# Hybrid encoder layer: a pair of token blocks re-ordered, first loads split around a wait, waits on one engine folded

## The reference

```python
proj = x @ w_in                       # conv GLU | q | k | v | q_mem | gate logits
y_conv = conformer_conv(glu_in, ...)  # GLU, depthwise conv of 31, LayerNorm, silu, projection
y_attn = windowed_gqa(q, k, v, ...)   # 8 heads, +-128 tokens, bias, sink -> projection
y_mem  = memory_attention(q_mem, mem, w_mem_kv) @ w_mem_out
merged = g0 * y_conv + g1 * y_attn + g2 * y_mem          # g = sigmoid(gate logits + b)
x = layer_norm(ALPHA * x + merged @ w_o, ln1_g, ln1_b)
gate, up = split(x @ w_ffn_in)        # 1024 -> 2 x 2816
x = layer_norm(ALPHA * x + (silu(gate) * up) @ w_ffn_out, ln2_g, ln2_b)
```

## Time and profile before

| what | value |
|---|---|
| runs | 978.34, 979.25, 1060.41 us, median 979.25 |
| profiled execution | 978.15 us, of which the slowest core's span is 977.1 us and 1.05 us lie around it |
| spans of the 8 cores | 975.5 to 977.1 us |
| TensorE matmul busy | 932.3 us, 95% of the span |
| VectorE | 632.1 us, 65% |
| ScalarE | 436.6 us, 45% |
| GpSimd | 256.1 us, 26% |
| chain that ended last | 84% TensorE, 5% VectorE, 4% issue, 3% DMA |

### The profile page before, as it was taken

One profiled execution on the slowest core, in us unless ns is written; L12 is line 12 of the kernel. 1 busy time (PEld: TensorE's weight loads), 2 busy tenths in 40 slices (PEclk: granted clock), 3 DMA queues, 4 the chain that ended last, 5 costly groups with the idle time before them and its releaser, 6 DMA issues.

```text
span 977.1 us, 16482 instructions; the slowest of 8 cores (975.5 to 977.1 us)
## 1 busy us (share of the span) xinstructions
PE 932.3 (95%) x5405; PEld 437.2 (45%) x5501; DVE 632.1 (65%) x1050; ACT 436.6 (45%) x719; POOL 256.1 (26%) x280
## 2 busy tenths in 40 slices
PE   4999999999999999999999999999999999999895
PEld 1455544544444444444445444444444444444342
DVE  1323575666766857566668798966575676675776
ACT  1125657575663354444556467654001444442121
POOL 3200000112135334334332355434100233332000
PEclk9999999999999999999999999999999999999998
DMA  8997033474249999622487277775533323221312
GB/s 131 184 172 140 24 86 95 82 129 72 45 72 138 113 149 126 84 66 54 90 254 272 62 173 168 137 184 122 170 129 108 108 88 111 89 81 37 115 44 87
DMA packets 39684, 112.13 MB, mean 115 GB/s; under 512 B 4976, under 2 KB 16888, under 8 KB 38608
## 3 DMA queue, kind: packets, MB, share of 16 engines
q0 software_dynamic: 11104, 41.16, 29.5%
q1 hardware_dynamic: 28496, 69.91, 23.3%
HBM read 132.49 MB, written 30.47 MB: 167 GB/s over the span
## 4 chain that ended last, share of the span: by engine, by line
PE 84%; DVE 5%; issue 4%; DMA 3%; ACT 3%; POOL 1%; DVEq 0%; ACTq 0%; POOLq 0%; SPq 0%
PE ps L233 82%; DMA arena<-xt 2%; DMA arena<-w_bf_cache 1%; ACT arena L597 1%; ACT arena L645 1%; DVE arena L1446 1%; PE ps L1276 1%; DVE arena L1209 1%; POOL arena L147 0%; DVE arena L1509 0%; DVE arena L590 0%; DVE arena L1483 0%; ACT arena L600 0%; PE ps L760 0%; ACT arena L1191 0%
## 5 line engine op out<-in xcount | busy, mean ns | idle before, releaser
L233 PE MATMUL ps<-arena 128*128 128x512 bf16 (+5 forms) x4995 | 914.3, 358 | 34.5 <-DMA arena<-xt 13.9
L233 PEld LDWEIGHTS ps<-arena 128*128 128x128 bf16 (+2 forms) x5091 | 417.0, 98 | 516.3 <-issue 74.4
L1325 ACT COPY arena<-ps 128x512 f32<-128x512 f32 x132 | 76.3, 586 | 132.3 <-PE ps L233 132.2
L1335 POOL TENSOR_TENSOR arena<-arena 128x512 bf16<-128x512 f32 x66 | 89.0, 1349 | 143.2 <-DVE arena L1328 137.5
L1328 DVE TENSOR_TENSOR arena<-arena,ps 128x512 f32<-128x512 f32 x132 | 88.2, 684 | 39.1 <-PE ps L233 38.7
L940 POOL TENSOR_TENSOR arena<-arena 128x512 f32<-128x512 f32 (+1 forms) x48 | 63.9, 1338 | 104.2 <-DVE arena L931 104.2
L1191 ACT ACTIVATE arena<-arena 128x1024 bf16<-128x1024 f32 x26 | 27.5, 1058 | 95.5 <-DVE arena L1620 88.5
L931 DVE SCALAR_TENSOR_TENSOR arena<-arena,ps 128x512 f32<-128x512 f32 x72 | 49.2, 684 | 23.9 <-ACT arena L927 18.0
L1205 POOL TENSOR_TENSOR rs<-mvt,eps_t 128x1 f32<-128x1 f32 x32 | 24.7, 771 | 144.5 <-DVE mvt L1201 91.9
L923 DVE TENSOR_TENSOR arena<-arena,ps 128x512 f32<-128x512 f32 x54 | 37.0, 686 | 35.3 <-ACT arena L920 19.7
L920 ACT COPY arena<-ps 128x512 f32<-128x512 f32 x54 | 31.6, 585 | 55.8 <-PE ps L233 55.8
(11 more groups left out here) (118 smaller groups left out, 573.2 us busy)
## 6 DMA issues: line engine op xcount, KB each, us to landing
arena<-w_bf_cache SPq DMA_DIRECT2D x44, 512.0 KB, 4.5
arena<-u_scratch SPq DMA_DIRECT2D x64, 135.0 KB, 3.4
arena<-x SPq DMA_DIRECT2D x16, 512.0 KB, 13.6
y_scratch<-arena SPq DMA_DIRECT2D x16, 512.0 KB, 6.2
arena<-y_scratch SPq DMA_DIRECT2D x16, 512.0 KB, 5.4
out<-arena SPq DMA_DIRECT2D x15, 512.0 KB, 2.6
arena<-w_f POOLq DMA_DIRECT2D x22, 256.0 KB, 5.0
arena<-w_g POOLq DMA_DIRECT2D x9, 512.0 KB, 20.5
```

The source lines that it names most:

```text
L233: return pe.run(lambda: nc.tensor.matmul(out, lhsT, rhs, start=start, stop=stop, skip_group_check=onto), deps, inc)
L1325: return act.run(lambda: nc.scalar.copy(buf, ps[:, b, :]), deps)
L1335: return pool.run(lambda: nc.gpsimd.tensor_tensor(out=dst, in0=up, in1=gate, op=ALU.mult), deps)
```

## The change

Four edits; the work that is computed stays the same.

1. `wait` first reduces the list of tokens: of one engine, or one DMA slot, only the largest stays, and one semaphore instruction is issued for it.
2. GpSimd issues only glu(0,1) and xt 0, then does its memsets and masks, then waits until glu(0,1) has landed, and then issues the other nine loads in the same order.
3. Of block 9 only the add and the squares stay in `f2_block`; the tiny steps (`small`), `center` and `scale` become three items of `fill`, and `form_T4(6, 11)` becomes the fourth, ahead of the six sums.
4. In the last pair the order p1, p2, p6, p5, p3, p7 becomes p1, p5, p2, p6, p3, p7. Block 14's row passes are split: center stays on VectorE and is put ahead of p7's `acc`; the scaling goes to ScalarE (an Identity with a scale, 128x1024, f32), the addition of the table to GpSimd (128x1024, f32).

```diff
     def wait(self, deps):
+        last = {}
         for tok in _flat(deps):
+            k = id(tok[1] if tok[0] == "E" else tok[0])
+            if k not in last or last[k][-1] < tok[-1]:
+                last[k] = tok
+        for tok in last.values():
...
     load_glu(0, 1)
     load_xt(0)
-    load_glu(0, 0)
-    load_glu(1)
-    load_xt(1)
-    load_glu(2)
-    load_glu(3)
...
     t_vm1 = pool.run(lambda: nc.gpsimd.memset(vm129[:, :, :, 128:129], 1.0))
+
+    pool.wait([t_glu[0, 1]])
+    load_glu(0, 0)
+    load_glu(1)
+    load_xt(1)
+    load_glu(2)
+    load_glu(3)
...
+        if last:
+            z, r5 = p5()
+            filler(1)
+        p2()
+        filler(2 if last else 1)
+        r6 = p6()
+        if not last:
+            filler(2)
+            z, r5 = p5()
         filler(3)
...
             stats(tb)
+            center, scale = pair_rows(tb)
+            center()
             p7()
             t = r8 = acc(Xb, L, x, [hb_tok[tb + 1]])
             banks.release(x, t)
-            for f in pair_rows(tb):
-                f()
+            t_row = act.run(lambda: nc.scalar.activation(Xa, Xa, AF.Identity, scale=rs16[:, 16 + tb:17 + tb]),
+                            [pair_tok["y", tb, 0], pair_tok["rs", tb]])
+            t_row = pool.run(lambda: nc.gpsimd.tensor_tensor(out=Xa, in0=Xa, in1=ln2t[1], op=ALU.add), [t_row])
+            dma(sp, out_d[tb * 128:(tb + 1) * 128, :], Xa, s_out[tb % 3], [t_row])
             w, dw = banks.alloc(1)
...
     f2_block(8)
     form_T4(0, 6, mid_done)
-    form_T4(6, 11, mid_done)
-    rows = [f2_block(9)]
+    rows = f2_block(9) + [lambda: form_T4(6, 11, mid_done)]
     counts = (1, 1, 2, 1, 2, 2)
```

More of the change, by code:

```diff
@@ L1541, in f2_pair, with p2, p6, p5 @@
         filler(0)
[L1542 to L1554, removed]
+        def p2():
+            y, dy = banks.alloc(1)
+            t = product(y, lambda j: actT[11 + j][:, a], lambda j: w2[11 + j][:, L], True, [dy])
+            t = acc(Xa, L, y, [t, r1], 1.0, sm[tb][0])
+            banks.release(y, t)
+            h[tb] = [t]
+            square(tb, 0, Xa, L, t)
+        def p6():
+            t = product(x, lambda j: S[:, 1, j], lambda j: T2[:, j], False, [r1, forms("T2"), sa["2"]])
+            return acc(Xa, H, x, [t, hb_tok[tb]])
+        def p5():
+            z, dz = banks.alloc(1)
+            t = product(z, lambda j: S[:, 0, j], lambda j: T1j[j], True, [dz, forms("T1"), sa["1a"], sa["1b"]])
+            return z, acc(Xb, H, z, [t, hb_tok[tb + 1]])
+        if last:
[7 more added lines that the diff above has]
+            z, r5 = p5()
         filler(3)
@@ L1614, in pair_rows @@
         return out
+    f2_t = {}
     def f2_block(tb, hooks={}):
@@ L1624, in f2_block, with small, center, scale @@
         t_st2 = ln_stats(xb, [t_h], tb)
[L1625 to L1630, removed]
+        def small():
+            t3 = f2_t["var", tb] = ln_tiny(t_st2, tb, hsum[:, 1, tb:tb + 1], 0)
+            f2_t["rs", tb] = ln_rstd(t3, tb, rs16[:, 16 + tb:17 + tb])
+        def center():
+            f2_t["y", tb] = ln_center(xb, ln2t[0], tb, [f2_t["var", tb], e_state["ln2"]])
+        def scale():
+            t_ln = ln_scale(xb, xb, rs16[:, 16 + tb:17 + tb], ln2t[1], [f2_t["rs", tb], f2_t["y", tb]])
             hb_free[r] = [dma(sp, out_d[tb * 128:(tb + 1) * 128, :], xb, s_out[r], [t_ln])]
@@ L1633, in rows @@
                 load_hb(tb + 3)
-        if tb in (7, 9):
-            return rows
-        rows()
+        if tb == 9:
+            return [small, center, scale]
+        small()
+        if tb == 7:
+            return lambda: (center(), scale())
+        center()
+        scale()
     def y_stores():
```

## The result

The changed kernel takes 972.42 us (median of 5 runs, 971.61 to 973.03), the kernel before 979.19 us (median of its runs beside them). The ratio is 0.9935 [0.9921, 0.9950]: 6.4 us faster by the ratio, 5 to 8 by its interval, which counts as the same within 2%. Forecast were 972.8 us and a range of 969.0 to 976.5. Runs in which the cores of a die fall behind, as in the 1060.41 us of the kernel before, are left out of every ratio.

The account below looks back on a forecast made before the run. TensorE was taken as the bound, the least helped core setting the time: core 1's 976.1 us less 2.89 + 0.9 + 0.9 gives 971.4, plus 1.05 around the span 972.5; forecast 972.8 us, range 969.0 to 976.5.

Parts of the forecast that it names:

- Pair 10's pause: TensorE's 2.89 us wait for r1 until 919.62 us disappears once form_T4(6, 11) and block 9's passes move: -2.89 us.
- the margin at p3: In pair 10, r5 ends 0.3 us before p3 needs it at 923.85 us, so no new pause.
- The clock: Slow matmuls behind pair 10's pause, at granted clock 0.52, regain full speed: -1.51 us, but not on core 1.
- The last pair: Reordered end with block 14's scaling and addition off VectorE: the 1.76 us pause goes, partly returned; -0.9 us, bounds 0.8 to 1.1.
- my case with a held t6: At the end, t6 starts only behind GpSimd's addition, at 21.3, ending at 26.55 us from p1's start; 0.8 us gained.
- the case that I preferred: At the end, t6 runs free at 19.8; GpSimd's addition holds block 15's center halves; end at 26.3 us against 27.3.
- The folded waits: Ahead of d_mm(0), ten wait tokens become three, cutting 1.22 us of TensorE idling: -0.9 us.
- The first loads: At the start, nine loads issue 2.7 to 3.4 us later behind queued DMA bytes, order unchanged: 0 us.
- Last pair gives nothing: Rival: GpSimd's addition is itself held up, ending at 22.75, so the last pair ends 1.3 us later: 974.1 us; 10%.
- Main point fails: Rival: r1 or r5 of pair 10 is still late and the clock falls again: 975 us; 8%.
- first loads later: Rival: the first loads land later by their issue, 3.3 us: 976.1 us; 8%.
- The rival on the slower side: Without long pauses TensorE runs unbroken from 487 us and is granted less clock; 0.015 lower gives 988 us; 4%.

Follow-up runs that it names:

- Block 9's edit: Kernel before with only block 9's tiny steps and row passes and form_T4(6, 11) moved to fillers of pair 10: 974.33 us, ratio 0.9961.
- dummies in the convolution: Changed kernel plus three unused matmuls in each of two TensorE pauses near 220 us: 971.98 us; first three only, with block 14's scaling on VectorE: 976.03 us.

## Why the prediction was right

**Pair 10's pause, -2.89 us.** It held, and was worth a little more. r1 needs no wait, TensorE has one piece of 359 matmuls, and the margin at p3, put at 0.3 us, sufficed: r5 came at 923.31 without a pause behind it. The pause was 2.89 us on every core before, so every core got it back. It was worth 3.05 us: the idle time of a row counts from the end of the last matmul, which is 0.38 us long by its record, while the next one otherwise starts 0.216 us behind its start. Core 1 of before:

```profile
916.54 0.81 PE L233 MATMUL ps<-arena 128*128 128x512 bf16 x3
920.24 0.59 PE L233 MATMUL ps<-arena 128*128 128x512 bf16 x2 [2.89 <-DVE arena L1509]
```

The third of these matmuls starts at 916.97, and 920.24 - 916.97 - 0.216 = 3.05.

**The clock, -1.51 us.** Right, and for core 4, from which it was read, right in size: from r1 to r1 that core took 33.91 us, 1.52 more than the 32.39 of a core that kept its clock. But core 4 got off lightly. Its clock was down already before the matmuls began again at 919.62 (TensorE alone, as in the earlier trace rows; no matmul, granted clock 0.64):

```profile
919.20:919.62 0.42, 0.00 (x0) 0.64 0.00 0
```

On 16 of the 25 cores that lost it the fall cost 1.64 to 1.69 us, on seven whose clock was down earlier 1.32 to 1.56, and on two, with two falls in a row, 2.95. Block 9's edit shows both terms together. From the last F1 addition to r1 of pair 10 it takes 3.6 us away (19.11 + 3.34 before, 17.71 + 1.14 after); from r1 to r1 1.14 (34.08 to 32.94). The sum is 4.74, and 3.05 + 1.69 = 4.74 for the two effects.

**The last pair, -0.9 us.** That the pause goes and part of it comes back was right. The term was mis-sized, -1.55 measured and outside of both its bounds (0.8 and 1.1), and of its two cases the one that I did not take came about. In the count from the start of p1, which is 2.9 us before r1 and so at 945.7 on core 3 after:

- GpSimd's addition ran from 18.4 to 20.7 and not from 18.65 to 21.2. It started 0.3 us sooner: VectorE's center pass took 961.36 - 960.16 = 1.20 us to the start of the next `acc` where I had laid out 1.35, the squares took 0.63 us where I had 0.8, and ScalarE's scaling 1.13 instead of 1.045. It lasted 2.34 us, not twice 1.28.
- t6 could start at 19.25 (I had 19.8), and it was slowed, until 20.7. My price for a held t6 let it start behind the addition and then added its own time; it ended together with the addition. That is another 0.25 us.
- From t6's end to the end of the core it was 4.9 us, against 5.1 before.

Together 0.3 + 0.2 + 0.25 + 0.15 = 0.9 us: from the 26.55 of my case with a held t6 down to 25.65, which against 27.3 is 1.65 (core 4 of before, whose last stretch was 24.4) or 1.5 against the 24.25 of the others. In the case that I preferred t6 was free and the center halves of block 15 were held; in fact t6 was held and they ran behind the addition at 0.70 each.

The Trainium skill's page "SBUF — State Buffer", section "SBUF: two separate sides", says that the two engines exclude each other for the whole of such instructions. The trace agrees for steps of one element per partition as well: t6 took 1.46 us beside the addition and ended with it, 0.16 without it, and the step at L1534 1.71 instead of 0.22.

**The folded waits, -0.9 us.** Measured 0.92 by itself, and the same 0.92 in the whole change on the six cores whose clock stayed up in that stretch. The chain of waits of core 3 has the remaining gap:

```profile
487.80 0.33 issue
```

**The first loads, 0.** Measured 0 by themselves; the issue of the nine loads is indeed later, and xt 1 isn't. The issue I had for core 4 (6.0, measured 6.07 in the change); that glu(0,1) lands by then on every core was wrong, and cost nothing.

**The sum.** 4.75 + 1.55 + 0.92 = 7.2 us for a core that had lost its clock at 917, and 3.1 + 1.55 + 0.92 = 5.6 for core 1, which had not; forecast were 6.2 and 4.7. The medians of the eight spans, 976.3 and 969.0, are 7.3 apart. The slowest spans, 977.1 and 971.4, are only 5.7 apart, and 971.4 is what I had forecast, but for another core and for another reason. By the measured terms core 1 would have come out at 976.1 - 5.6 = 970.5 as the slowest; it came out at 968.9, because before it had also lost 1.7 us at 222 and this time it had not. The slowest is core 3, by a double fall of the clock at 223 us, which I had not looked for although three cores of before have a single one. Against its own row of before, core 3 gained 0.5 us up to the GLU step, lost 2.3 up to `d_mm` (0.9 gained by the waits, 3.2 lost to the clock), gained 0.8 in `d_mm` and the first FFN product, most of it (0.6) a stall at 641 us that this run has not, and 6.3 at the end: 5.3 in all. So the total is right by luck, by two errors that offset one another: terms about 0.9 to 1.0 too small, and a term missing that costs the slowest core more than that. The range too is wider than its working: from 972.8 the three sources named for its lower end (1.7, 0.3 and 0.2 us) lead to 970.6 and not to 969.0.

**The rivals.** "Last pair gives nothing": GpSimd's addition took 2.34 us, so it was not held. "Main point fails" and "first loads later" did not come about. The rival on the slower side, a lower clock because the pauses are gone, is refuted (its 0.015 of clock would also have been 14 us, so 987 and not 988): 209 of 209 us are busy at 1.00, and the mean clock of the cores is 0.994 to 0.997 where it was 0.993 to 0.996.

**Left open.** Why one core and not another loses the clock after the same pause. In the profiles of the eleven kernels without dummies in the convolution, before and after among them, 26 of 88 cores lost it near 222 us; with the dummies 0 of 16. On the two chips that the dummies ran on it was 10 of 40 without them. In all 16 the pause of 0.70 us still stood, and only that of 0.78 was filled. So the idling of the first pause has a part in it; what else decides isn't known.

## What to carry to other kernels

Once all cores run the same program at almost the same time, the slowest core sets it, and a gain on each of them arrives only in part where some rare loss (here a fall of the clock at 222 us, 1.7 us each, 3.3 for two in a row) hits at least one core of eight in most runs; cut the traces into stretches by instructions that both kernels have, and compare all cores, before a median is explained. A pause of TensorE costs the time from start to start (0.16 us more than the idle time of its row) and perhaps the slow stretch behind it: with half of the pause removed no core lost its clock, and dummy products do it as well where the wait itself has to stay, if they stand in the pause and not behind it. And before work is given to GpSimd to relieve VectorE, look at what VectorE does beside it, tiny steps too, and at what stands behind it on GpSimd: a gap on VectorE itself was the better place (0.77 us).

## What was not expected of the hardware

- VectorE steps of one element per partition with two SBUF inputs took 1.46 and 1.71 us beside a 128x1024 f32 addition on GpSimd, 0.16 and 0.22 without it. One with a single SBUF input, `TENSOR_SCALAR` at L1537, took 0.21 us while the same addition ran.
- After the pause of 2.89 us 25 of 32 cores ran on at a granted clock near 0.5, which cost 1.32 to 1.69 us, and 2.95 on two of them. After a pause of 1.49 us none of 8 did, nor did any of the 8 cores of before behind the 1.76 us of the last pair. In the convolution, behind 0.78 and 0.70 us with narrow matmuls of six rows or columns between them, 26 of 88 did.
- Ten semaphore instructions ahead of a matmul take 1.22 us in the chain, three 0.33 us; each is 0.051 us long by its own record.
- The start is spread by more than most terms here: over all these kernels the first matmul comes at 10.1 to 14.2 us and the last GLU step at 172.2 to 178.1 us.
